# A two-layer diffusion block in FP32: lag products, power buffers and the output product reordered

## What is computed

```python
def merge_branches(p, y_s, w_four, w_glu_a, w_glu_b, w_out):
    g_a = sigmoid(p[..., OFF_GA:OFF_GB])
    g_b = sigmoid(p[..., OFF_GB:])
    y_a = fourier_mix(p[..., :OFF_SSM]) @ w_four
    y_b = (y_s @ w_glu_a) * sigmoid(y_s @ w_glu_b)
    return (g_a * y_a + g_b * y_b) @ w_out

def token_mixer(...):
    p = a @ w_in                      # Fourier input, scan input, gates a and b
    y = s5_branch(p[scan input], ...) # bidirectional complex diagonal scan, then gelu
    return merge_branches(p, y, w_four, w_glu_a, w_glu_b, w_out)

def reference(...):
    for l in range(2):
        h = h + g1 * token_mixer(l, rmsnorm(h) * (1 + sc1) + sh1)
        h = h + g2 * channel_mixer(l, rmsnorm(h) * (1 + sc2) + sh2)
    return rmsnorm(h, final_g)
```

## Time and profile before

| | us |
|---|---|
| median of three runs | 2124.06 (2121.07 to 2124.74) |
| the profiled execution | 2135.39 |
| its span in the trace | 2133.5 |
| PE busy in it | 2050.1 (96%) |
| DVE busy | 1372.9 (64%) |
| ACT busy | 920.0 (43%) |

### The profile page before, as it was taken

One profiled execution on the slowest core, in us unless ns is written; L12 is line 12 of the kernel. 1 busy time (PEld: TensorE's weight loads), 2 busy tenths in 40 slices (PEclk: granted clock), 3 DMA queues, 4 the chain that ended last, 5 costly groups with the idle time before them and its releaser, 6 DMA issues.

```text
span 2133.5 us, 24374 instructions
## 1 busy us (share of the span) xinstructions
PE 2050.1 (96%) x10010; PEld 1535.7 (72%) x10010; DVE 1372.9 (64%) x1845; ACT 920.0 (43%) x839; POOL 0.2 (0%) x4
## 2 busy tenths in 40 slices
PE   6999898999999999999989999999999999999997
PEld 2446363447777777578877888888888888888885
DVE  7585644662232333246247898898989888898986
ACT  3202112121221221111116777767776776677774
POOL 0000000000000000000000000000000000000000
PEclk9999999989999999999988999999999999999998
DMA  8532775332435442268526999999998999999993
GB/s 365 128 144 99 196 247 181 116 108 111 166 138 217 166 160 85 96 185 198 178 119 262 371 355 370 340 359 368 358 374 329 374 360 366 355 342 372 359 373 134
DMA packets 83838, 529.27 MB, mean 248 GB/s; under 512 B 23056, under 2 KB 49552, under 8 KB 52752
## 3 DMA queue, kind: packets, MB, share of 16 engines
q1 hardware_dynamic: 62976, 508.65, 64.7%
q10 hardware_dynamic: 20752, 19.05, 2.6%
HBM read 509.39 MB, written 18.28 MB: 247 GB/s over the span
## 4 chain that ended last, share of the span: by engine, by line
PE 89%; DMA 5%; DVE 3%; ACT 1%; issue 1%; SPq 1%; DVEq 0%; ACTq 0%
PE ps L1621 21%; PE ps L1976 14%; PE ps L1961 14%; PE ps L1962 14%; PE ps L1630 6%; PE ps L1634 6%; PE ps L1637 6%; PE ps L1564 2%; DMA bps<-BWs 2%; PE ps L1783 1%; PE ps L1907 1%; DMA ring<-in_w_mod 1%; DVE WL L1450 1%; PE ps L1890 1%; PE ps L1791 1%
## 5 line engine op out<-in xcount | busy, mean ns | idle before, releaser
L1450 DVE TENSOR_TENSOR WL<-mring,WH 128x2048 fp32r<-128x2048 f32 x336 | 755.1, 2288 | 108.7 <-ACT WH L900 108.6
L900 ACT ACTIVATE WH<-mring 128x2048 fp32r<-128x2048 f32 x336 | 626.1, 1913 | 145.2 <-PE ps L1976 102.4
L1961 PE MATMUL ps<-WH,XGh 128*128 128x512 f32 x896 | 355.6, 397 | 2.4 <-ACT WH L900 2.4
L1962 PE MATMUL ps<-WH,XGl 128*128 128x512 f32 x896 | 351.0, 392 | 0.0
L1621 PE MATMUL ps<-aT,ring 128*128 128x512 f32 (+1 forms) x768 | 272.7, 516 | 4.1 <-ACT aT L779 4.1
L1621 PEld LDWEIGHTS ps<-aT,ring 128*128 128x128 f32 x768 | 147.5, 194 | 123.7 <-issue 112.6
L1976 PE MATMUL ps<-WL,XGh 128*128 128x512 f32 x896 | 221.6, 389 | 0.0
L1961 PEld LDWEIGHTS ps<-WH,XGh 128*128 128x128 f32 x896 | 169.2, 189 | 36.7 <-issue 2.5
L1962 PEld LDWEIGHTS ps<-WH,XGl 128*128 128x128 f32 x896 | 169.2, 189 | 34.1
L1976 PEld LDWEIGHTS ps<-WL,XGh 128*128 128x128 f32 x896 | 168.2, 188 | 35.0
L1259 DVE TENSOR_TENSOR ringl<-ring,FWH 128x4096 fp32r<-128x4096 f32 (+2 forms) x19 | 73.4, 3864 | 183.0 <-ACT FWH L765 183.0
(11 more groups left out here) (259 smaller groups left out, 2080.5 us busy)
## 6 DMA issues: line engine op xcount, KB each, us to landing
mring<-in_moe_gate SPq DMA_DIRECT2D x56, 2048.0 KB, 9.8
mring<-in_moe_up SPq DMA_DIRECT2D x56, 2048.0 KB, 9.7
mring<-in_moe_down SPq DMA_DIRECT2D x56, 2048.0 KB, 9.6
ring<-in_w_mod SPq DMA_DIRECT2D x24, 2048.0 KB, 8.1
ring<-in_w_in SPq DMA_DIRECT2D x12, 2048.0 KB, 12.0
ring<-in_ffn_gu SPq DMA_DIRECT2D x11, 2048.0 KB, 10.8
cks<-CW ACTq DMA_DIRECT2D x16, 512.0 KB, 3.2
ring<-cks SPq DMA_DIRECT2D x4, 2048.0 KB, 12.4
```

Source lines behind the costliest of these rows:

```text
L900: nc.scalar.activation(WH[buf][:, o], mring[t % MRING][:, o], ACT.Copy).then_inc(high_done, 1)
L1450: V.tensor_tensor(WL[buf][:, o], mring[t % MRING][:, o], WH[buf][:, o].bitcast(F32), ALU.subtract).then_inc(low_done, 1)
L1961: mm(out_, ah, WH[buf][:, o:o + 512], start=(first and q == 0), stop=False)
L1962: mm(out_, al, WH[buf][:, o:o + 512], start=False, stop=False)
```

## The change

It has four parts.

1. **Lags.** PE does `lags(0, 0)` and `lags(0, 1)` straight after dft2, ahead of `mod_sums(8)`, and then one `lags(0, m + 2)` behind each gb m up to m = 5. ACT's queue is rewritten to match: `store_reads` and `masked` for n = 0 and 1 ahead of gb, then one of each per gb. `store_lags(0, 0)` moves from ahead of gb 3 to behind gb 4, `store_lags(0, 1)` from behind gb 4 to behind gb 6, and the load of `raw` for layer 1 from behind gb 4 to behind gb 5.
2. **Turned powers.** A second buffer `BW1` (in the memory of `H`), used by the odd n; the semaphore `bw_stored` becomes two. `turned(1, n)` waits for the store n - 2 instead of n - 1.
3. **Output product.** The wait for eight mixed blocks becomes a wait for one block ahead of each K step of the first output product, in both layers.
4. **GLU tile.** In layer 1 the load of `w_glu_b` stands ahead of the two "ys" moves in SP's list instead of behind them.

```diff
@@ -154,7 +154,7 @@
         powers_made = sem("powers_made")
-        bw_stored = sem("bw_stored")
+        bw_stored = [sem(f"bw_stored{i}") for i in range(2)]
         c_made = sem("c_made")
@@ -279,8 +279,8 @@
         stream += [("w_in", 1, n) for n in (2, 3, 4, 5)]
-        stream += [("toep", 1, 0), ("ck", 1, 0), ("ck", 1, 1), ("w_four", 1, 0), ("ys", 1, 0), ("ys", 1, 1)]
-        stream += [("w_glu_b", 1, 0), ("w_glu_a", 1, 0), ("w_out", 1, 0), ("w_out", 1, 1)]
+        stream += [("toep", 1, 0), ("ck", 1, 0), ("ck", 1, 1), ("w_four", 1, 0), ("w_glu_b", 1, 0), ("ys", 1, 0), ("ys", 1, 1)]
+        stream += [("w_glu_a", 1, 0), ("w_out", 1, 0), ("w_out", 1, 1)]
         moves = stream
@@ -368,6 +368,9 @@
         prep.close()
+        turns = ExitStack()
+        BW1 = sb(turns, "BW1", [P, 4, 2, P])
+        turns.close()
         H = sb(mix, "H", [P, NCH + 1, 2, 32])
@@ -531,7 +534,8 @@
                 if key[0] == "bp":
-                    sp.wait_ge(bw_stored, 16 * 4 * (key[2] + 1))
+                    for b in range(2):
+                        sp.wait_ge(bw_stored[b], 16 * 2 * (key[2] + 1))
                 if key[0] == "ck":
@@ -674,7 +678,8 @@
                 if l == 1 and n == 1:
-                    act.wait_ge(bw_stored, 16 * ITS)
+                    for bw in bw_stored:
+                        act.wait_ge(bw, 16 * ITS // 2)
                 if n >= 2:
@@ -685,18 +690,19 @@
                 mh, q = n // 4, n % 4
-                if l == 1 and n:
-                    act.wait_ge(bw_stored, 16 * n)
+                BW = (BWs, BW1)[n % 2]
+                if l == 1 and n >= 2:
+                    act.wait_ge(bw_stored[n % 2], 16 * (n // 2))
                 for r in range(2):
                     bank, free = arrived(act, ("turn", l, n, r))
-                    dst = GR[:, SLOT * mh + D * q:SLOT * mh + D * q + D] if l == 0 else BWs[:].rearrange("p g r c -> p (g r c)")
+                    dst = GR[:, SLOT * mh + D * q:SLOT * mh + D * q + D] if l == 0 else BW[:].rearrange("p g r c -> p (g r c)")
                     nc.scalar.activation(dst.rearrange("p (g r c) -> p r g c", g=4, r=2)[:, r],
...
                         taken(act, ("turn", l, n, r))
-                    act.dma_start(bps[mh][:, D * q:D * q + D], BWs[:].rearrange("p g r c -> p (g r c)"))\
-                        .then_inc(bw_stored, 16)
+                    act.dma_start(bps[mh][:, D * q:D * q + D], BW[:].rearrange("p g r c -> p (g r c)"))\
+                        .then_inc(bw_stored[n % 2], 16)
@@ -819,21 +825,23 @@
                 if l == 0:
+                    for i in range(2):
+                        store_reads(0, i)
+                        masked(0, i + 2)
                     mod_rows(8)
                 for m in range(8):
-                    if l == 0 and m == 3:
+                    evac(("gb", l, m), G2[:, m, t0:NT], ACT.Sigmoid, n)
+                    if l == 0 and m + 2 < ITS:
+                        store_reads(0, m + 2)
+                    if l == 0 and m + 4 < ITS:
+                        masked(0, m + 4)
+                    if l == 0 and m == 4:
                         store_lags(0, 0)
-                    evac(("gb", l, m), G2[:, m, t0:NT], ACT.Sigmoid, n)
-                    if l == 0 and m < 4:
-                        for i in range(2 * m, 2 * m + 2):
-                            store_reads(0, i)
-                        for i in range(2 * m + 2, 2 * m + 4):
-                            if i < ITS:
-                                masked(0, i)
-                    if l == 0 and m == 4:
-                        store_lags(0, 1)
+                    if l == 0 and m == 5:
                         act.wait_ge(b_masked, 2 * ITS)
                         act.dma_start(raw[:].rearrange("p a r c h -> p (a r c h)"), a["bc"][1]).then_inc(raw_in, 16)
+                    if l == 0 and m == 6:
+                        store_lags(0, 1)
                     if l == 0 and m == 5:
@@ -1170,7 +1178,8 @@
                     if l == 1:
-                        dve.wait_ge(bw_stored, 16 * ITS)
+                        for bw in bw_stored:
+                            dve.wait_ge(bw, 16 * ITS // 2)
                 if n >= 2:
@@ -1747,6 +1756,8 @@
                 if l == 0:
+                    lags(0, 0)
+                    lags(0, 1)
                     mod_sums(8)
@@ -1754,11 +1765,10 @@
                                     [(w[:, k, P * m:P * m + P], aT[:, k, t0:NT]) for k in range(KD)], n_)
-                            if l == 0 and h == 0:
-                                if m == 0:
-                                    mod_turn(8)
-                                lags(0, 2 * m)
-                                lags(0, 2 * m + 1)
+                            if l == 0 and (h, m) == (0, 0):
+                                mod_turn(8)
+                            if l == 0 and 4 * h + m < ITS - 2:
+                                lags(0, 4 * h + m + 2)
                             if l == 0 and (h, m) == (1, 1):
@@ -1814,12 +1824,12 @@
                     mod_turn(11)
-                pe.wait_ge(mix_ready, 8 * l + 8)
                 for h in range(2):
...
                         product(("out", l, 4 * h + m),
-                                [(w[:, k, P * m:P * m + P], G[:, k, t0:NT]) for k in range(KD)], n_)
+                                [(w[:, k, P * m:P * m + P], G[:, k, t0:NT]) for k in range(KD)], n_,
+                                blocks=(mix_ready, 8 * l) if h + m == 0 else None)
                         if l == 0 and 1 <= 4 * h + m <= 4:
```

## The result

| | forecast | measured |
|---|---|---|
| the changed kernel, median | 2118.7 us (2109 to 2125.5) | **2137.57 us** (2135.93 to 2140.13, 4 runs) |
| the kernel before, median of the same session | | 2123.86 us |
| ratio | 0.9975 | **1.0051** [1.003, 1.0071] |
| span in the trace | 2128.1 | 2133.9 |

By the ratio the change makes the kernel 11 us slower (6 to 15); the medians lie 13.7 us apart. The two profiled executions are alike in length only because that of before was a long one, 11 us over its median, and that of after is not.

The account below looks back on a forecast made before the run. PE was taken as the bound, busy 2050.1 of 2133.5 us, with time won only at stops or lower clock. Part 1's +10.3 less 3.6, 1.7, 6.4 and 4.0 gave -5.4 us: 2118.7 us, range 2109 to 2125.5.

Parts of the forecast that it names:

- +1.7 us for the clock: Layer 0, Y: clock loss of 1.7 us charged behind the 11 us stop for the late toep loads.
- 15.7 for parts 2 to 4: Gains forecast for output product (3.6 and 1.7), turned powers (6.4) and GLU tile (4.0), in us.
- A charge of 1.7 us for each stop of 1.9 us or more: Any PE stop that long was taken to cost 1.7 us of lower clock behind it, besides its length.
- store 5 held behind SP's loads: Layer 0, end of gb 3: store 5 takes 16.0 us beside two 2 MB loads, stopping PE 5.3 us.
- the two signs: The prediction is wrong if Y's second half starts before 286, or glub still shows a stop for ACT.
- part 2's 6.4 us: Glub, layer 0: the second buffer removes the 4.82 us stop for ACT and 1.6 us of clock loss.
- part 4's 4.0 us: Layer 1: the earlier GLU tile load removes a 2.19 us stop and 1.78 us of clock loss.
- store 5 was starved: Rival said store 5 is not starved and powers 7 are ready in time: 2111.6 us, chance 0.16.
- toep was late: Rival said toep loads finish within 10.7 us of their start, so Y is not held: 2106.0 us, chance 0.06.
- SP's later loads didn't slow it: Rival said ck and w_four, issued by SP, delay toep by 10 us: 2128.7 us, chance 0.08.
- the glub stop went: Rival said another wait holds ACT in glub and 6.4 us are lost again: 2125.1 us, chance 0.08.

Follow-up runs that it names:

- part2: The kernel before with the second buffer for turned powers alone: 2122.45 us against 2127.68, ratio 0.998.
- part34: The kernel before with the early w_glu_b load and the wait per out product alone: 2117.76 us, ratio 0.9962.
- the third profile of before: The kernel before run once more, unchanged, for another profile: 2127.18 us, ratio 0.9999.
- the second profile: The kernel before run once more, unchanged, for another profile: 2130.33 us, ratio 1.0017.
- parts234: The changed kernel with the gb loop, lags and stores of the kernel before: 2116.88 us against 2127.68, ratio 0.9953.
- gap: The kernel before with 12 chained ACT copies that PE waits for ahead of Y, a stop of 1.16 us: 2139.39 us against 2128.8, ratio 1.0063.
- part1: The kernel before with the first part of the change alone (lags and stores): 2145.57 us, ratio 1.009.
- fill: best with 7 unused 512-column products ahead of its wait for toep: 2109.46 us, ratio 0.9919.
- split_fill: best with toep loaded in two halves, each waited for separately, and 3 unused products ahead of the wait for the second ck: 2108.72 us, ratio 0.9919.
- fill3: best with 3 unused 512-column products ahead of its wait for toep: 2119.76 us.
- best: The changed kernel with store 5 behind gb 2, lags 5 to 7 a product earlier and both gds stores behind gb 4: 2122.64 us, ratio 0.9978.

## Why the prediction was wrong

- **The step that failed is the term "+1.7 us for the clock" behind the stop in Y.** It measured 15.7 us: 42.0 against 26.4 in the table. The size came from the earlier trace rows, where the work behind the stop is products of 256 and 512 columns; there the clock is back after a loss of 1.7 us in all. Behind the stop in Y come 64-column matmuls, and they kept PE busy for 28 us at 1.2 GHz until ya 0, with its 512 columns. The rows were read rightly, but they were of other work. With 15.7 in place of 1.7 the sum of the prediction is +8.6, and with 10.8 in place of 15.7 for parts 2 to 4 it is +13.5; the medians give +13.7 (6 to 15 by the ratio).
- A charge of 1.7 us for each stop of 1.9 us or more was no rule elsewhere either. Behind the stop of 3.2 us at the lags, the gate product took 8.83 us in three of the kernels that keep that order (*part2*, *part34*, the third profile of before), 9.46 and 9.40 in two (the second profile, *parts234*), and 7.13, no loss, in *gap*. The stop of 2.25 us in E cost nothing.
- The mechanism of part 1 up to the stop was right to 2 us: store 5 held behind SP's loads (16.1 us, forecast 16.0), a stop of 5.12 us at the last lags (5.3), Y at 266.21 (267.1), toep issued at 261.62 (263.7), Y's lag half at 283.43 (285.4). Toep took 21.8 us (21.7). That Y's second half starts at 290.45, where 290.8 was forecast, is luck: toep came 2.0 us early and the half clock made the lag half 3.3 us longer, where 1.7 had been charged. Neither of the two signs that the prediction named for being wrong came up: neither looks at the pace of Y behind the stop.
- Parts 2 to 4: 15.7 us forecast, 10.8 measured together (6 to 13), 5.2 and 9.9 apart. By the ratios the two are 4.3 and 8.1 us against 10.0 together, which their intervals cover. Two terms were sized on stops that not every execution has: part 2's 6.4 us (the stop in glub is in two of three profiles of before, and in none of *gap*, *part1* and *part34*, which have one buffer too) and part 4's 4.0 us (2.19 + 1.78 in the first profile, 1.66 and 1.30 in the others).
- The forecast took gains seen against a profiled execution of 2135.4 us off a median of 2124.1, though other executions may lack these stops.
- Rivals: store 5 was starved, toep was late, SP's later loads didn't slow it (the second ck caused no wait in after), the glub stop went. So none of the four came true; the loss came from a case that had no chance of its own, a clock that does not come back.
- Toep took 21.8 us again. By the 512 B and the 358 GB/s of the Trainium skill (DMA: Bandwidth & Descriptors, Specifications) it would have been some 6 us, an estimate from that page, so the trace goes on disagreeing with it. Whether the size of the pieces sets the rate, or for instance that each of the eight loads goes to 16 partitions only, no run shows.

## What to carry to other kernels

Price a stop of TensorE by what runs behind it. In this mixer a stop of 1.3 to 5.1 us ahead of 256- or 512-column products cost its length and 0 to 2.3 us. One of 1 to 10 us in Y, ahead of 64-column matmuls that last 11 to 15 us at full clock, cost its length and 10 to 16 us more. So either leave no stop there, or put dense work behind it or into it. And look for a row of the same kind of work before a price is carried over: the stop in E shows that 64 columns alone do not tell, and at the start of the feed-forward of before, behind stops of 1.64 and 2.00 us, even 512-column products ran at a granted clock of 0.50 from 467 to 483 us, while the weight loads for them waited 3.5 us for ACT and 3.3 us for DVE to make operands.

The 2 us of slack that before had ahead of Y's lag half were worth more than the stops that the change removed. And take a second profile of the kernel before its stops are counted as gains: one execution may have a stop that the next has not.

## What the runs showed of the hardware

- At full clock PE passed from products to the 64-column matmuls and kept 2.4 GHz through all of Y (before, *fill*, *split_fill*). After each stop of 0.84 to 9.94 us ahead of or between them it ran at 1.2 GHz, at once or after up to 2.6 us at the full clock (an estimate from 11.65 us in *fill3*, where full clock gives 7.41 and half clock 13.92), and did not come back in up to 28 us of unbroken work, until 512-column matmuls ran. The stop of 0.31 us in *fill3* left the 3.79 us behind it as they were. Whether the width does it, or that nearly every matmul here brings a weight load of its own (PEld busy 26.76 of 27 us in *gap*), the runs don't separate; the number of rows does not, since the matmuls on H with 64 rows and those on the lag matrices with 128 both took nearly twice their time. The Trainium skill (TensorE: Matmul & The Clock Gate, The HAM clock gate) says that the clock is set by how busy PE has been recently. By that alone Y's second half in the gap kernel would have been back at 7.41 us; it took 13.92, and the window behind the stop has 27.00 us busy of 27 at 0.51, so the measurement decides.
- A store of 512 KB on ACT's queue that was issued together with two 2 MB loads on SP's took 15.8 to 16.1 us in three kernels, and 3.8 one gate product earlier.
- Work that nobody reads made the kernel faster by 13 us (*fill* against *best*, 2109.46 to 2122.64).
